# Second half of the output projection with tokens on the partitions, six raw weight buffers, and weight loads issued by ScalarE, in a fp32r decoder block

## The chip, the core and the metric

One Trainium2 chip, one core. The metric is the device time of one execution of the program, in microseconds (us). The kernel before takes 1840.0 us, the median of three runs (1839.93, 1840.0 and 1843.25). The engines are TensorE (PE, with PEld for its weight loads), VectorE (DVE), ScalarE (ACT), GpSimd (POOL) and SyncE (SP, which here only issues transfers).

## What is computed

One decoder block on 1024 tokens of width 2048, in float32. The input projection has 6528 columns; they feed an RWKV-7 group (16 heads, a recurrence over tokens) and a sliding-window attention group (16 heads). Their gated outputs are concatenated (2048 wide), go through the output projection, are added to x, and a final RMSNorm runs over the 2048 channels of each token. Cut to what matters here:

```
h = rmsnorm(x, norm_gain)
proj = h @ w_in                                   # 2048 x 6528
y_rwkv = rwkv7_group(proj[..., :4224], ...)
y_attn = swa_sink_alibi_group(proj[..., 4224:], sinks)
mix = concatenate([y_rwkv, y_attn])               # 1024 x 2048
x = x + mix @ w_out                               # 2048 x 2048
return rmsnorm(x, final_gain)
```

## The kernel before, in words

Tokens are worked on in two halves of 512. Everything is channel-major: channels lie on the 128 partitions, tokens on the free axis. A projection is cut into column tiles of 128 channels (51 for each half of the input projection, 16 for each half of the output projection, 134 in all), and each tile into four quarters of the contraction. One quarter is one weight piece of 128 x 512 (256 KB) and 12 matmuls of 512 columns: each fp32 product is made of three fp32r products (high x high, high x low, low x high), so both x and the weights are split into a rounded high part and the remainder. There are 536 quarters, numbered gq in the order in which PE takes them; 4 phases (input projection of half 0 and 1, output projection of half 0 and 1) begin at quarters 0, 204, 408 and 472. Constants: `START` is 12, `base(j)` the first quarter of interval j (24 quarters; 16 intervals, one per pair of heads and half), and `at` the quarter counted from there.

All engines run the same loop over gq, each through its own list of instructions, and are coupled by semaphores alone:

- SP (`load_w`, L365 to L370) issues the load of quarter gq+6 into one of three raw buffers. It waits until VectorE has made the low part of the piece that lay there (`w_ready`). SP also issues all other loads and stores, in program order with these.
- ScalarE (`high`, L581) makes the rounded part of quarter gq+4: it waits for the landed piece (`w_landed`) and for a free pair of split buffers, five of them, so it is at most four quarters ahead of PE (`w_used`).
- VectorE (`low`, L806) makes the remainder (`w_ready`), PE (`quarter`, L1230) waits for it.
- Between these stand the other parts of the block: `channels(j, at)`, `recurrence(j - 1, at)`, and `slices`, which split the x of a new phase (L587, L811) in groups of four chunks every second quarter. Around the state recurrence, `chain` (at 20 to 24) alternates between a small matmul on PE (L1511) and a copy on ScalarE (L729 to L733), eight times in an interval.

At the start, PE needs the mean square of the tokens of half 0: ScalarE squares x rows (L598), VectorE spreads the sums (L866), PE multiplies by a matrix of 1/2048 (L1523, at quarter 11), ScalarE takes the root (L610), VectorE the reciprocal (L872), and only then can tiles be read out of PSUM. At quarter 15 PE multiplies by the small LoRA matrices (L1263), which need the tanh of the first tile (L619); ScalarE's two sigmoids of these products (L632, L635) stand at quarter 14 of its list, and PE's transposes of the value tile (L1228, quarter 16) wait for the second.

At the end of each half of the output projection the 16 tiles (128 channels x 512 tokens) are read out and added to x (`add`, L1147), squared on ScalarE (L740), summed on GpSimd (L554 to L556) and over partitions on PE, and scaled (L1161) and stored. For half 1 this stands behind the last matmul: square, column sums by 8 matmuls (L1544), root (L747), reciprocal, a turn back to channel layout (L1228), 16 scalings and 16 stores.

## Time and profile before

| | |
|---|---|
| median of three runs | 1840.0 us (1839.93 to 1843.25) |
| the profiled execution | 1838.38 us, of which the span is 1836.5 us |
| PE busy | 1806.4 us (98%) |
| DVE busy | 1240.2 us (68%) |
| ACT busy | 814.6 us (44%) |
| POOL busy | 481.6 us (26%) |
| mean granted TensorE clock | 0.996 |
| DMA, mean | 115 GB/s |

The page's first part gives busy time and share per engine. The timeline lists instructions in order of time: start, duration, engine, line, operation, tiles, count; in brackets stands how long the engine had been idle before it and what released it. A large matmul stands with 0.39 us, but the next starts about 0.23 us later: matmuls overlap, so spacing is read from starts. A name with q (SPq, ACTq, DVEq) is an engine's instruction queue: there an issue of a transfer occupies the queue for the time given.

### The profile page before, as it was taken

The page shows a single profiled execution, that of the slowest core. Times are in us where ns is not written, and L with a number is a line of the kernel's source. Part 1 is how long each engine was busy: PE and PEld are TensorE (multiplying, and loading weights), DVE is VectorE, ACT ScalarE, POOL GpSimd, SP SyncE. Part 2 cuts the span into 40 slices and gives each one's busy share as a digit, 9 for nine tenths or more (in the row PEclk, how much of TensorE's full clock was granted, in tenths as well). Part 3 has the DMA queues.
Part 4 walks back from the last instruction along what each step waited for, and adds up shares of the span by engine and source line. Part 5 has one row for each costly group of instructions (what it writes and reads, how often), then busy time and mean ns, then how long its engine had stood idle before and what let it go on. Part 6 is the DMA issues. An engine that isn't in the chain of part 4 may idle for free.

```text
span 1836.5 us, 37316 instructions
## 1 busy us (share of the span) xinstructions
PE 1806.4 (98%) x14530; PEld 1482.5 (81%) x14530; DVE 1240.2 (68%) x2240; ACT 814.6 (44%) x1682; POOL 481.6 (26%) x1096
## 2 busy tenths in 40 slices
PE   8999999999999999999999999999999999999996
PEld 6878888888888887888888888888888888888885
DVE  5876777776767777567777767777778764356433
ACT  7544435353535355444453535353544543242221
POOL 0014233241505060232332515060605051111110
PEclk9999999999999999999999999999999999999998
DMA  8633333333333335332333333333334543465443
GB/s 299 196 97 90 89 93 91 94 95 94 91 90 92 92 93 171 114 95 86 95 88 95 97 90 92 89 97 89 106 90 116 167 113 114 124 210 179 154 120 126
DMA packets 197840, 211.84 MB, mean 115 GB/s; under 512 B 98592, under 2 KB 103840, under 8 KB 197152
## 3 DMA queue, kind: packets, MB, share of 16 engines
q1 hardware_dynamic: 196800, 208.73, 39.6%
q8 instruction: 115, 1.88, 0.4%
q10 hardware_dynamic: 864, 0.73, 0.1%
q14 instruction: 61, 0.50, 0.1%
HBM read 187.37 MB, written 22.02 MB: 114 GB/s over the span
## 4 chain that ended last, share of the span: by engine, by line
PE 90%; DVE 3%; DMA 2%; POOL 1%; ACT 1%; issue 1%; SPq 0%; DVEq 0%; ACTq 0%; POOLq 0%
PE psum L1243 75%; PE psum L1228 3%; PE psum L1361 2%; PE psum L1301 2%; PE psum L1329 1%; PE psum L1511 1%; PE psum L1394 1%; PE psum L1475 1%; DMA work<-in_x_t 1%; PE psum L1482 1%; PE psum L1263 1%; POOL sub_t L534 1%; POOL sub_io L536 1%; PE psum L1464 1%; DVE w_lo L808 1%
## 5 line engine op out<-in xcount | busy, mean ns | idle before, releaser
L1243 PE MATMUL psum<-x_hi,w_hi 128*128 128x512 f32 x2144 | 864.5, 403 | 10.5 <-DVE x_lo L817 6.2
L1243 PE MATMUL psum<-x_hi,w_lo 128*128 128x512 f32 x2144 | 838.7, 391 | 0.0
L1243 PE MATMUL psum<-x_lo,w_hi 128*128 128x512 f32 x2144 | 838.2, 391 | 0.0
L808 DVE TENSOR_TENSOR w_lo<-w_raw,w_hi 128x512 fp32r<-128x512 f32 x536 | 376.2, 703 | 477.3 <-ACT w_hi L579 449.3
L579 ACT ACTIVATE w_hi<-w_raw 128x512 fp32r<-128x512 f32 x536 | 335.5, 629 | 734.0 <-PE psum L1243 639.2
L1243 PEld LDWEIGHTS psum<-x_hi,w_hi 128*128 128x128 f32 x2144 | 403.4, 188 | 105.9 <-DVE w_lo L808 10.1
L1243 PEld LDWEIGHTS psum<-x_hi,w_lo 128*128 128x128 f32 x2144 | 402.8, 188 | 87.5
L1243 PEld LDWEIGHTS psum<-x_lo,w_hi 128*128 128x128 f32 x2144 | 403.8, 188 | 76.8 <-issue 0.7
L534 POOL TENSOR_TENSOR sub_t<-sub_l,sub_io 128x60 f32<-128x60 f32 (+24 forms) x496 | 192.1, 387 | 850.5 <-DMA sub_l<-scratch_L 812.9
L536 POOL TENSOR_TENSOR sub_io<-sub_io,sub_t 128x60 f32<-128x60 f32 (+24 forms) x496 | 209.7, 423 | 38.9
L556 POOL TENSOR_TENSOR v<-v,kb 128x512 f32<-128x512 f32 x29 | 38.1, 1314 | 267.1 <-ACT kb L740 266.7
L579 ACT ACTIVATE states<-psum,pc 128x64 f32<-128x64 f32 x112 | 35.0, 313 | 95.2 <-PE psum L1511 95.0
L579 ACT ACTIVATE late<-psum 64x256 f32<-64x256 f32 (+2 forms) x128 | 58.2, 482 | 1.1
L1511 PEld LDWEIGHTS psum<-states,score 128*128 128x128 f32 x256 | 47.9, 188 | 12.6 <-ACT states L579 1.9
L660 ACT ACTIVATE score<-score,top 128x192 f32<-128x192 f32 x128 | 56.5, 443 | 2.6 <-DVEq L1016 1.6
L933 DVE RECIPROCAL work<-work 128x512 f32<-128x512 f32 x16 | 53.6, 3353 | 2.2
L826 DVE TENSOR_TENSOR raw<-psum,rms 128x512 f32<-128x512 f32 x68 | 46.7, 686 | 3.4
L1511 PE MATMUL psum<-states,score 128*128 128x64 f32 x256 | 42.4, 247 | 0.7 <-ACT states L579 0.5
L984 DVE TENSOR_TENSOR late<-psum,cst 128x512 f32<-128x512 f32 x64 | 41.1, 684 | 2.4
L525 POOL COPY sub_io<-sub_ident 128x256 f32<-128x256 f32 x16 | 6.5, 406 | 125.3 <-PE psum L1403 107.0
L999 DVE SCALAR_TENSOR_TENSOR score<-cst,psum 128x192 f32<-128x192 f32 x128 | 36.6, 348 | 3.4 <-DVE ym L1138 3.4
L842 DVE SCALAR_TENSOR_TENSOR work<-work,par,raw 128x512 f32<-128x512 f32 x48 | 36.1, 752 | 1.7
(249 smaller groups left out, 1833.7 us busy)
## 6 DMA issues: line engine op xcount, KB each, us to landing
w_raw<-in_w_in SPq DMA_DIRECT2D x408, 256.0 KB, 2.7
w_raw<-in_w_out SPq DMA_DIRECT2D x128, 256.0 KB, 2.7
sub_l<-scratch_L SPq DMA_DIRECT2D x16, 384.0 KB, 4.1
stage<-in_x_t SPq DMA_DIRECT2D x20, 256.0 KB, 4.4
stage<-scratch_MIX SPq DMA_DIRECT2D x19, 256.0 KB, 4.0
late<-in_x_t SPq DMA_DIRECT2D x16, 256.0 KB, 3.7
scratch_MIX<-sa SPq DMA_DIRECT2D x16, 256.0 KB, 3.5
scratch_MIX<-ym SPq DMA_DIRECT2D x16, 256.0 KB, 3.2
```

The lines of the kernel that those rows point to most:

```text
L534: then(nc.gpsimd.tensor_tensor(t, left, right, ALU.mult))
L536: then(nc.gpsimd.tensor_tensor(rows, rows, t, ALU.subtract))
L556: then(nc.gpsimd.tensor_tensor(c_acc[:], c_acc[:], c_sq[u % 2], ALU.add))
L579: return nc.scalar.activation(dst, src, ACT.Copy, scale=scale)
L660: nc.scalar.activation(prob[:, x], prob[:, x], ACT.Exp, bias=top[:, 1, x:x + 1], accum_out=top[:, 2, x:x + 1])
L808: nc.vector.tensor_tensor(w_lo[gq % SPLIT][:], w_raw[gq % RAW][:], w_hi[gq % SPLIT][:].bitcast(F32), ALU.subtract).then_inc(w_ready, 1)
L826: then(nc.vector.tensor_tensor(dst, psum[:, bank_of(s)], rms[s // H1][:], ALU.mult))
L933: then(nc.vector.reciprocal(grow, grow))
L984: ins = nc.vector.tensor_tensor(am[:, 2 * half:2 * half + 2, hh].rearrange("p b c x t -> p b (c x t)"), psum[:, bank].rearrange("p (b t) - ...
L1228: return nc.tensor.transpose(dst, src, const("ident"))
L1243: mm = nc.tensor.matmul(psum[:, bank_of(s)], wt[gq % SPLIT][:, cols], xx[:, c], start=(c == 0 and wt is w_hi and xx is x_hi), stop=(c == K ...
L1511: nc.tensor.matmul(psum[:, 6, m * HD:(m + 1) * HD], mt[:, m], states[:, m], start=False, stop=True, skip_group_check=True).then_inc(state_ ...
```

## The change

Five edits come together.

1. Weight loads. From the fourth tile on (quarter 12 and later) ScalarE issues them, in its own list, ahead of `high(gq + 4)`. SP keeps the loads of the first three tiles. From quarter `WIDE` (492) on there are six raw buffers instead of three (the three staging buffers of x are then free), and loads are issued nine quarters ahead. What each load waits for is the low part of quarter gq+3 in either case.
2. The output projection of half 1 has tokens on the partitions: x is now the 128 x 128 stationary operand, and 512 columns of w_out move. Units are (column block of 512, chunk of the contraction): three passes of 16 units with four token blocks (12 matmuls each) and two passes of 16 units with two token blocks (6 matmuls each), so 80 units in place of 64 quarters, with 768 matmuls as before. A row's sum of squares comes from the accumulator of ScalarE's Square; root and reciprocal are on 128x1 columns; the gain row is multiplied on GpSimd for three column blocks.
3. x of phases 1 to 3 is split in pairs of chunks every quarter, in place of four chunks every second one.
4. The mean matmul of half 0 stands ahead of quarter 12 in place of quarter 11.
5. In the recurrence: the 32 matmuls of L1464 and L1467 are issued in two rounds of four, each in the order `TURNS`. And VectorE reads the R tile (`evicted`) ahead of the products that wait for `kkt_full`, not behind them.

The diff, cut to its core:

```diff
+ROWS = 4 * OUT1
+PASSES = [(cb, range(TBS)) for cb in range(CBS - 1)] + [(CBS - 1, (0, 1)), (CBS - 1, (2, 3))]
+LAST_UNITS = 4
+QUARTERS = ROWS + KC * len(PASSES)
+ADDED_AT = [ROWS + KC * (at + 1) + 1 + 2 * i for at, (_, tbs) in enumerate(PASSES[:-1]) for i in range(len(tbs))]
+FIRST_SCALED = ADDED_AT[-1] + 1
+WIDE, WIDE_RAW = 3 * ((ROWS + KC) // 3 + 1), 6
...
+        def loaded_by(gq):
+            return min(QUARTERS - 1, gq + 6 + (WIDE_RAW - RAW if gq + 6 >= WIDE + RAW - 1 else 0))
...
             @block.sync
                 for gq in range(QUARTERS):
-                    if START <= gq + 6 < QUARTERS:
-                        load_w(gq + 6)
...
             @block.scalar
+                def load_w(gq):
+                    slot = raw_of(gq)[0]
+                    if gq >= WIDE + WIDE_RAW:
+                        act.wait_ge(w_ready, gq - WIDE_RAW + 1)
+                    elif slot >= RAW:
+                        act.wait_ge(x_ready, 4 * KC)
+                    else:
+                        act.wait_ge(w_ready, gq - RAW + 1)
...
+                    nc.scalar.dma_start(w_raw[slot][:], src).then_inc(w_landed[slot], 16)
...
+                    for ahead in range(loaded_by(gq - 1) + 1, loaded_by(gq) + 1):
+                        if ahead >= START:
+                            load_w(ahead)
                     if START <= gq + 4 < QUARTERS:
                         high(gq + 4)
...
+                    if gq in ADDED_AT:
+                        square_rows(ADDED_AT.index(gq))
+                    if gq == FIRST_SCALED:
+                        root_rows(0)
+                        root_rows(1)
+                    if gq - FIRST_SCALED in (1, 2):
+                        scale_rows(gq - FIRST_SCALED - 1)
+                for tb in (2, 3):
+                    square_rows(PIECES.index((CBS - 1, tb)))
+                    root_rows(tb)
+                    scale_rows(tb)
...
             @block.vector
+                def add_rows(n):
+                    cb, tb = PIECES[n]
...
+                    nc.vector.tensor_tensor(row_piece[tb][cb], psum[:, row_bank(cb, tb)], x_in[n % 2], ALU.add
+                                            ).then_inc(row_read, 1)
...
             @block.tensor
-                    if gq == START - 1:
+                    if gq == START:
...
+                def row_products(gq, tb, c, cb):
...
+                    nc.tensor.matmul(psum[:, bank], x_hi[:, c, tokens], hi[:], start=(c == 0), stop=False)
+                    nc.tensor.matmul(psum[:, bank], x_hi[:, c, tokens], lo[:], start=False, stop=False)
+                    return nc.tensor.matmul(psum[:, bank], x_lo[:, c, tokens], hi[:], start=False, stop=(c == KC - 1))
```

How instructions stand on the engines, in three places. First ScalarE's list near the start, from the last two squares of x rows to the root of the first mean (`rms0`); w_raw and w_hi with their numbers are the raw and the rounded weight buffers, `late` the squared x rows. Before:

```order
L598 ACTIVATE work,stat<-work 128x2048
L598 ACTIVATE late,stat<-late 128x2048
L579 ACTIVATE w_hi2<-w_raw0 128x512
L579 ACTIVATE w_hi3<-w_raw1 128x512
L610 ACT_TABLE_LOAD
L610 ACTIVATE rms0<-psum,eps 128x512
L579 ACTIVATE w_hi4<-w_raw2 128x512
```

and in the changed kernel, whose line numbers differ:

```order
L682 ACTIVATE late,stat<-late 128x2048
L662 DMA w_raw0<-in_w_in 128x512
L662 DMA w_raw1<-in_w_in 128x512
L662 DMA w_raw2<-in_w_in 128x512
L646 ACTIVATE w_hi2<-w_raw0 128x512
L662 DMA w_raw0<-in_w_in 128x512
L646 ACTIVATE w_hi3<-w_raw1 128x512
L694 ACT_TABLE_LOAD
L694 ACTIVATE rms0<-psum,eps 128x512
L662 DMA w_raw1<-in_w_in 128x512
L646 ACTIVATE w_hi4<-w_raw2 128x512
L662 DMA w_raw2<-in_w_in 128x512
```

The loads of quarters 12 to 14 stand behind the last square of x rows, and from quarter 15 on one load stands ahead of each rounding.

Second, ScalarE's list in the last pass of the output projection, where the sums of squares (`row_sums`), their roots (`stat`) and the first scalings come between the roundings of the weights. Before, the last tiles of half 1:

```order
L579 ACTIVATE w_hi0<-w_raw2 128x512
L579 ACTIVATE w_hi1<-w_raw0 128x512
L579 ACTIVATE w_hi2<-w_raw1 128x512
L579 ACTIVATE w_hi3<-w_raw2 128x512
L740 ACTIVATE kb<-score 128x512
L579 ACTIVATE w_hi4<-w_raw0 128x512
```

and in the changed kernel:

```order
L836 ACTIVATE kb,row_sums<-wr 128x512
L662 DMA stage1<-in_w_rows 128x512
L646 ACTIVATE w_hi2<-stage2 128x512
L662 DMA stage2<-in_w_rows 128x512
L646 ACTIVATE w_hi3<-w_raw0 128x512
L836 ACTIVATE kb,row_sums<-sub_io 128x512
L662 DMA w_raw0<-in_w_rows 128x512
L646 ACTIVATE w_hi4<-w_raw1 128x512
L841 ACTIVATE stat<-stat,eps 128x1 x2
L662 DMA w_raw1<-in_w_rows 128x512
L646 ACTIVATE w_hi0<-w_raw2 128x512
L646 ACTIVATE xt<-xt,stat 128x512
```

A load stands between each two roundings, and it waits for VectorE's remainder of the piece that was rounded just before it.

Third, VectorE's list at quarter 196 and 197 (the last interval of half 0), where `raw` is the buffer into which the R tile is read. Before:

```order
L808 TENSOR_TENSOR w_lo0<-w_raw2,w_hi0 128x512
L936 SCALAR_TENSOR_TENSOR work<-work,par 128x512
L938 TENSOR_TENSOR qr<-work,decay 128x4x64 x2
L826 TENSOR_TENSOR raw<-psum,rms0 128x512
L838 COPY carry<-raw 128x1
L808 TENSOR_TENSOR w_lo1<-w_raw0,w_hi1 128x512
```

and in the changed kernel:

```order
L921 TENSOR_TENSOR w_lo0<-w_raw2,w_hi0 128x512
L939 TENSOR_TENSOR raw<-psum,rms0 128x512
L951 COPY carry<-raw 128x1
L1051 SCALAR_TENSOR_TENSOR work<-work,par 128x512
L1053 TENSOR_TENSOR qr<-work,decay 128x4x64 x2
L921 TENSOR_TENSOR w_lo1<-w_raw0,w_hi1 128x512
```

The read of the tile has moved ahead of three instructions.

## Rows read from the trace of the kernel before

**Rows 1.** The page's first part: busy us, share, instructions.

```profile
PE 1806.4 (98%) x14530; PEld 1482.5 (81%) x14530; DVE 1240.2 (68%) x2240; ACT 814.6 (44%) x1682; POOL 481.6 (26%) x1096
```

**Rows 2.** Timeline of PE, where it waits: start, us, line, operation [idle before].

```profile
39.82 0.67 PE L1523 MATMUL psum<-v,cst 128*128 128x512 f32 x1 [1.80 <-DVE v L866]
...
693.73 0.50 PE L1243 MATMUL psum<-x_hi,w_hi 128*128 128x512 f32 x1 [2.81 <-DVEq L830]
...
712.11 0.44 PE L1511 MATMUL psum<-states,score 128*128 128x64 f32 x2 [0.51 <-ACT states L579]
...
1419.65 0.50 PE L1243 MATMUL psum<-x_hi,w_hi 128*128 128x512 f32 x1 [0.55 <-DVEq L830]
...
1642.97 0.50 PE L1243 MATMUL psum<-x_hi,w_hi 128*128 128x512 f32 x1 [0.92 <-DVE late L1147]
```

**Rows 3.** Timeline behind the last large matmul, PE, DVE, ACT and SP.

```profile
1817.90 0.39 PE L1243 MATMUL psum<-x_hi,w_lo 128*128 128x512 f32 x1
...
1818.33 0.69 DVE L1147 TENSOR_TENSOR pt<-psum,decay 128x512 f32<-128x512 f32 x1 [10.19 <-PE psum L1243]
1819.05 0.63 ACT L740 ACTIVATE kb<-pt 128x512 f32<-128x512 f32 x1 [10.25 <-DVE pt L1147]
...
1820.83 0.26 ACT L747 ACTIVATE part<-psum,eps 128x4 f32<-128x4 f32 x1 [1.14 <-PE psum L1544]
1821.12 0.18 DVE L1155 RECIPROCAL part<-part 128x4 f32<-128x4 f32 x1 [2.10 <-ACT part L747]
...
1823.02 0.75 DVE L1161 SCALAR_TENSOR_TENSOR xt<-xt,fgain,psum 128x512 f32<-128x512 f32 x1 [1.26 <-PE psum L1228]
...
1832.24 1.40 DVE L1161 SCALAR_TENSOR_TENSOR pt<-pt,fgain,psum 128x512 f32<-128x512 f32 x2
1833.01 0.99 SPq L473 DMA_DIRECT2D out<-pt  x2
```

**Rows 4.** Timeline of PE in the recurrence of interval 15.

```profile
1422.61 0.69 PE L1394 MATMUL psum<-zs,xt 64*64 64x64 f32 x32
1423.12 0.39 PE L1394 MATMUL psum<-kkt,xt 64*64 64x64 f32 x13
...
1426.65 0.36 PE L1464 MATMUL psum<-late,wr 64*64 64x64 f32 x8
...
1427.88 0.34 PE L1475 MATMUL psum<-late 128*64 128x64 f32 x4
```

**Rows 5.** Timeline near the start: one piece rounded, its remainder, the next load.

```profile
3.69 0.63 ACT L579 ACTIVATE w_hi<-w_raw 128x512 fp32r<-128x512 f32 x1 [1.01 <-DMA w_raw<-in_w_in]
...
4.36 0.69 DVE L808 TENSOR_TENSOR w_lo<-w_raw,w_hi 128x512 fp32r<-128x512 f32 x1 [2.68 <-ACT w_hi L579]
...
5.08 0.33 SPq L370 DMA_DIRECT2D w_raw<-in_w_in  x1
```

**Rows 6.** Timeline of ACT, DVE and PE, 37 to 56 us.

```profile
37.66 1.13 ACT L579 ACTIVATE w_hi<-w_raw 128x512 fp32r<-128x512 f32 x2
...
41.67 3.35 DVE L872 RECIPROCAL rms<-rms 128x512 f32<-128x512 f32 x1 [1.40 <-ACT rms L610]
...
51.16 1.28 ACT L632 ACT_TABLE_LOAD   x1
...
52.39 0.69 DVE L808 TENSOR_TENSOR w_lo<-w_raw,w_hi 128x512 fp32r<-128x512 f32 x1
...
53.49 0.68 ACT L635 ACTIVATE work<-psum,par 128x512 f32<-128x512 f32 x1
...
55.68 0.60 PE L1228 MATMUL psum<-cst,raw 128*128 128x128 f32 x4
```

**Rows 7.** The page's DMA issues: KB of one, median us from issue to landing.

```profile
w_raw<-in_w_in SPq DMA_DIRECT2D x408, 256.0 KB, 2.7
```

**Rows 8.** Waits of ACT and of SP's queue: us in total, times, longest.

```profile
ACT states L579 <- PE psum L1511: 95.0, 101, 1.3
...
SPq L370 <- DVE w_lo L808: 1216.2, 468, 7.3
```

More of the change, by code:

```diff
@@ L159, in slices_before, with row_bank @@
     return 1 + (i >= values_before(1)) + (i >= values_before(2))
+def row_bank(cb, tb):
+    return (0 if cb % 2 else 4) + tb
 def us_rows(c):
@@ L285, in program @@
                       pt[:, 0], pt[:, 1]]]
+        row_piece = [[xn[1][CBS * tb + cb] for cb in range(CBS)] for tb in range(TBS)]
+        row_inv = stat[:, 0, 0:TBS]
         psum = ctx.enter_context(nc.psum_tensor("psum", [P, 8, HALF], F32))
@@ L291, in program @@
         ident_landed = sem("ident_landed")
-        w_landed = [sem(f"w_landed{i}") for i in range(RAW)]
+        w_landed = [sem(f"w_landed{i}") for i in range(WIDE_RAW)]
         x_landed = [sem(f"x_landed{i}") for i in range(STAGE)]
@@ L352, in current, with chunk_pair @@
             return [(j, gq - base(j)) for j in range(INTERVALS + 1) if 0 <= gq - base(j) < TAIL]
-        def chunk_group(gq):
+        def chunk_pair(gq):
             for ph in range(1, 4):
-                group, odd = divmod(gq - (4 * FIRST[ph] - 6), 2)
-                if 0 <= group < 4 and not odd:
-                    return ph, group
+                pair = gq - (4 * FIRST[ph] - 6)
+                if 0 <= pair < KC // 2:
+                    return ph, 2 * pair, 2
             return None
@@ L557, in accumulate, with gain_rows @@
                     pool.sem_inc(c_summed, 1)
+                def gain_rows(cb):
+                    pool.wait_ge(row_gain_landed, 16)
+                    for tb in range(TBS):
+                        pool.wait_ge(row_squared, TBS * cb + tb + 1)
+                        piece = row_piece[tb][cb]
+                        nc.gpsimd.tensor_tensor(piece, piece, gain_row[:, cb * HALF:(cb + 1) * HALF], ALU.mult
+                                                ).then_inc(row_gained, 1)
                 nc.gpsimd.memset(xt[:], 0.0)
@@ L571, in _ @@
                                 clear(j - 1)
-                    for u in range(2 * KC - 1):
+                    for u in range(KC):
                         if gq == done(OUT0 + u) + 1:
                             accumulate(u)
+                    for at in range(CBS - 1):
+                        if gq == ROWS + KC * (at + 1):
+                            gain_rows(at)
             @block.scalar
@@ L788, in _ @@
                             channels(j, at)
-                    for u in range(2 * KC - 1):
+                    for u in range(KC):
                         if gq == done(OUT0 + u) + 1:
                             square(u)
-                    if gq == 4 * OUT1 + 5:
-                        root(0)
-                square(2 * KC - 1)
-                root(1)
+                    if gq == ROWS + 5:
+                        root()
+                    if gq in ADDED_AT:
[9 more added lines that the diff above has]
+                    scale_rows(tb)
             @block.vector
@@ L1536, in between @@
                                 chain(j - 1, 2 * (at - 20))
-                    quarter(gq, between)
-                pe.wait_ge(c_summed, 2 * KC - 1)
-                for last, squared in enumerate((c_acc[:], c_sq[(2 * KC - 1) % 2])):
-                    if last:
-                        pe.wait_ge(c_squared, 2 * KC)
-                    for b in range(NB):
-                        mm = nc.tensor.matmul(psum[:, 2, b:b + 1], squared[:, b * P:(b + 1) * P], const("mean")[:, 0:1],
-                                              start=(not last and b == 0), stop=bool(last), skip_group_check=True)
-                mm.then_inc(mean_done, 1)
-                pe.wait_ge(c_spread, 1)
-                for b in range(NB):
-                    mm = turn(psum[:, 3, b * P:(b + 1) * P], rms[0][:, b * P:(b + 1) * P])
-                mm.then_inc(c_turned, 1)
+                    if gq < ROWS:
+                        quarter(gq, between)
+                    else:
+                        rows(gq)
+                last_rows()
 SCRATCH = {
```

303 lines of the change are left out of this document (209 added, 94 removed).

## The prediction, made before the changed kernel was run

> **What bounds the kernel now.** I read the engines' shares first, then the places where PE waits, then the chain behind the last matmul, and last the rows of ScalarE and VectorE around the weight pieces. PE is busy for 1806.4 of 1836.5 us [rows 1], and large matmuls of the last phase start 0.228 us apart: (1817.90 - 1642.97) / 767 for its 768 [rows 2, 3]. So nothing that VectorE, ScalarE or a transfer does faster counts, unless PE waits for it. PE waits in few places: behind the start 1.80 us for the first mean, 2.81 and 0.55 us for a tile to be read at the end of each half's last interval, 0.51 us for a state copy, 0.92 us at the start of the last phase [rows 2]. The other idle time is at the end: the last matmul ends at 1818.3, the span at 1836.5, so 18.2 us hold one tile's way through add, square, sum, root and reciprocal, and then 16 scalings and stores [rows 3]. The question is thus which PE waits go, which ones come, and how long the end becomes. I work from the profiled execution, 1838.38 us, 1.6 us below the median of 1840.0, and add the 1.6 us at the end.
>
> **The end.** With tokens on the partitions the last unit leaves only four 128x512 pieces to finish, two of them already summed. Behind the last matmul: add 0.7 (L1147's 0.69), square with its accumulator 0.75 (L740's 0.63 and an estimated 0.1 for reading the sum), sum, root 0.26, reciprocal 0.18 and the hops between, 0.8 together, then two scalings on ScalarE, 1.2, beside two on VectorE: 3.5 us. SP issues each store in 0.33 (0.99 for the overlapping pair and wait at 1833.01), so the last of four issues starts at about 4.0; before, the last one started near 1833.67 and the span ended 2.8 later [rows 3]. That makes 6.8 us in place of 18.2: **-11.4**, with 5.8 to 8.5 as its bounds (landings side by side, or one issue behind another).
>
> **PE waits that go.** VectorE now reads the R tile straight behind the remainder of quarter 200, ahead of three instructions, and the load of that quarter is not stuck in SP's list, so I take both waits of 2.81 and 0.55 as gone; behind them PE next needs quarter 197's piece, long ready. The first pass of the last phase writes four fresh banks and doesn't wait for a tile to be added: 0.92 goes. Pairs of chunks halve the block of splits that held up the state copy: 0.51 goes. Together **-4.8** (bounds -3.4 to -4.8).
>
> **The recurrence.** The 32 matmuls of L1464 and L1467 take 1427.88 - 1426.65 = 1.23 us in each interval. They alternate pairs on the same 64x64 corner of the array. The 16 matmuls of L1394, issued in the order TURNS, take 0.51 [rows 4], so 32 would take 1.02. The difference of 0.21 times 16 intervals is **-3.4** (bounds 0 and -3.4).
>
> **Loads on ScalarE, in the middle.** An issue occupies a queue for 0.33 us [rows 5]: some 540 of them are 178 us more on an engine busy for 814.6 [rows 1], so there is room on average. What hurts is order. SP's queue waits 1216.2 us, in 468 waits, for remainders that VectorE has not yet made [rows 8]; this wait now stands in ScalarE's list, ahead of the rounding of quarter gq+4 and whatever follows. Laid side by side, the 536 roundings and remainders of before show that the remainder of quarter gq+3 is mostly done when ScalarE gets there; it is late by more than the issue at the fifth quarter of each interval (about 1.2 us, with over 2 us of ScalarE idling behind it) and at the 22nd of every fourth (1.2 to 1.6 us). In the state chain ScalarE waits for PE 0.94 us per copy (95.0 / 101) [rows 8], which covers the 0.33; and PE, once a copy is made, needs it only about 0.9 later. I take **0**, with 0 to +10 as bounds.
>
> The Trainium skill, page DMA: Bandwidth & Descriptors, section Issuing engines are not separate DMA queues, says that transfers issued by different engines run on the same 16 DMA engines and interleave; by that rule only issue time can be saved, which here is SP's, on which nothing waits, and the edit would be worth nothing. The row of 1216.2 us says more than the rule does: the wait moves as well.
>
> **The start.** Here the order costs. Before, SP issued the load of quarter 12 long before ScalarE needed it, and ScalarE rounded it at 37.66 right behind the last square [rows 6]. Now the load is issued behind that square, at about 36.9 (I assume that the queue is some 0.8 ahead of the engine), and lands 2.7 later [rows 7], at 39.7. Rounding and remainder (1.4) and the spreading of the sums (0.7) put the mean matmul at 41.9 in place of 39.82 [rows 2]. PE has quarter 11 to do meanwhile, so its wait is only about 1.1. The table load ahead of the root is no longer hidden: the reciprocal starts at 44.2, not 41.67, and ends 2.5 late. Behind it stand in VectorE's list the remainders of 14 and 15, the first tile, remainder 16, the keys, remainder 17. Before, remainder 17 ended at 53.08 [rows 6]; now it is 2.5 later, and 0.9 more, since the rounding of 15 stands behind a load that waits for remainder 14: 56.5. ScalarE's two sigmoids stand behind the load that waits for this one: issue 0.35, rounding 0.63, a square 0.6, table load 1.28, sigmoids 1.35: 60.7. PE's transposes of the value tile need the second sigmoid, and started at 55.68 [rows 6]; now 60.8: **+5.1**. The bounds are +1.4 (only the tanh ahead of quarter 15 late) and +8.
>
> **The last two passes.** A unit has six matmuls, 1.37 us. Its piece must be rounded, its remainder made, and now a load issued, before the next piece can be rounded, since the load waits for that remainder: from 3.69 to 5.41 us these three take 1.72 [rows 5], 1.75 with the hop back. So rounding, remainder and issue run one behind the other, slower than PE. Where VectorE adds a finished piece and ScalarE squares it, the step is 1.38 to the remainder, 0.6 for the add, 0.75 for the square: 2.7. Count from the start of unit 520, PE's first short one, when the piece of 524 is rounded: up to 544 there are 14 steps of 1.75 and 6 of 2.7 (four adds in the fourth pass, two in the fifth), 40.7 us. Roots and reciprocals make the next step 2.25, two scalings the next 1.8; the remainder of 547 stands behind VectorE's scalings and ends at 48.0, and the last four follow 0.6 apart: 50.4. PE would be at its last four units after 28 x 1.365 = 38.2 us. So it waits **+12.2** in small pieces from about the tenth short unit on. Bounds: 0, if ScalarE's issue and wait overlap with its work, and +16, if an issue takes 0.45 and a square 0.8. The lead of four pieces is in the count already. The three passes before have units of 2.74 us, above the mean of 1.75 and 2.7 to 3.6, and cost nothing.
>
> **Sum.** -11.4 - 4.8 - 3.4 + 5.1 + 12.2 = -2.3: 1836.1 by the profiled execution, 1837.7 as a median. Two large terms of either sign nearly cancel, which is why the range is wide.
>
> **Rivals.**
> 1. *The last passes don't run in step.* For it: no row of before shows ScalarE waiting at an issue in mid-stream, and VectorE is 68% busy only [rows 1]. Against it: the load stands ahead of the next rounding in the list, and waits for a remainder made only after the last one. It would give 1837.7 - 12.2 = 1825.5.
> 2. *The start stays covered.* If ScalarE's queue gets its loads out earlier, during the squares, the term of 5.1 shrinks to about 1: 1833.5. Against it: the three loads stand behind the last square, which starts only when its rows have landed.
> 3. *The state chain falls behind (slower).* Each interval has eight copies in a row on ScalarE, with a load and a rounding between them. If VectorE's remainders come so much later than now that a load holds ScalarE for more than the 0.94 us of slack in a copy [rows 8], PE waits in each interval; it decides from about 1 us of delay at one copy. Half a microsecond to one in 15 intervals is 7 to 15 us: 1845 to 1853, say 1848. For it: delays of 1.2 to 1.6 in three intervals already. Against it: there the copy would come some 0.8 late, still inside the slack.
>
> **Chances.** The forecast 0.52 (own range 1833.5 to 1842.5), rival 1 0.18, rival 2 0.12, rival 3 0.18. About 0.2%, 3.7 us, is what a measurement can tell from no change. Faster, below 1836.3: both first rivals mostly (0.27), and a fifth of the forecast: 0.38. Slower, above 1843.7: rival 3, and a twentieth of the forecast: 0.21. Same: 0.41. The range of 1826 to 1846 leaves out most of rival 3's upper part and half of rival 1.
>
> **What the new profile would show.** The end: 6 to 8 us between the last large matmul and the span's end. The start: the mean matmul near 42, the transposes of the value tile near 61 with 3 to 5 us of PE idle before them. The middle: no wait of more than 0.6 us for a tile read at the ends of the halves, 1.0 us for the 32 matmuls. The last two passes: a sum of PE waits for remainders of 10 to 15 us, roundings 1.75 us apart, each behind a load issue. I am wrong if PE has no gaps there (rival 1), or if PE waits for state copies in every interval (rival 3).

## The result, and the profile after

The changed kernel takes 1846.05 us, the median of nine runs (1845.61 to 1848.12), beside 1840.0 us before, the median of nine runs as well (1836.39 to 1843.25). The ratio is 1.0035, with 95% interval 1.0025 to 1.0045: 0.35% slower, where 1837.7 us had been forecast. The profiled execution took 1847.35 us; its span is 1845.2 us, 8.7 us longer than the 1836.5 before. The mean granted TensorE clock is 0.997, as before 0.996, so the difference is not one of the clock as a whole. The two profiled executions lie on opposite sides of their medians (1.3 us above it after, 1.6 us below it before), so what is read from the traces below adds up to 8.7 us where the medians are 6.1 us apart.

The busy times of the engines answer to [rows 1]:

```profile
PE 1811.9 (98%) x14510; PEld 1477.4 (80%) x14510; DVE 1252.5 (68%) x2254; ACT 840.0 (46%) x1725; POOL 479.2 (26%) x1093
```

PE's share is the same and says nothing. The places where it waits do. These are the waits of PE after (line and tile, what was waited for: us in total, times, longest):

```profile
PE psum L1668 <- DVE w_lo L921: 9.2, 20, 1.6
...
PE psum L1378 <- ACT work L719: 3.8, 1, 3.8
PE psum L1413 <- issue: 1.9, 1, 1.9
PE psum L1378 <- DVEq L1101: 1.3, 1, 1.3
PE psum L1434 <- DVEq L1070: 1.2, 1, 1.2
```

L1668 is the first of the three matmuls of a token block in the last phase (`row_products`), L1378 the transposes, L1413 the LoRA matmuls of quarter 15. The waits of [rows 2] (1.80, 2.81, 0.51, 0.55, 0.92 us) are not there any more. In their place stand 20 small waits for remainders in the last two passes, two at the start, of 1.9 us at L1413 (PE is done with quarter 14 at 51.4, and the tanh that it needs then ends at 53.1) and of 3.8 us for the second sigmoid, and two of just over 1 us later on, of which the one at L1434 had been 0.65 before.

To see what each is worth, I took the start of the same work on PE in both traces and subtracted: after minus before, in us.

| PE starts | shift |
|---|---|
| quarter 16 | +5.88 |
| quarter 17 | +8.08 |
| last phase (quarter 472) | +3.51 |
| last two passes (unit 520; before, the matmul 576 of the phase) | +3.34 |
| last large matmul | +18.87 |
| end of the span | +8.7 |

So the start costs 8.1, the whole middle gives back 4.6, the last two passes cost 15.5, and the end gives back 10.2.

**The start.** Timeline of all engines after, 36 to 61 us (start, duration, engine, line, tiles; in brackets the idle time before and what ended it); it answers to [rows 6]:

```profile
36.77 1.30 ACTq L662 DMA_DIRECT2D w_raw<-in_w_in  x3
...
39.64 0.63 ACT L646 ACTIVATE w_hi<-w_raw 128x512 fp32r<-128x512 f32 x1 [0.93 <-DMA w_raw<-in_w_in]
...
41.81 1.10 PE L1711 MATMUL psum<-v,cst 128*128 128x512 f32 x2
...
44.20 3.35 DVE L985 RECIPROCAL rms<-rms 128x512 f32<-128x512 f32 x1 [1.31 <-ACT rms L694]
```

```profile
56.86 0.34 ACTq L662 DMA_DIRECT2D w_raw<-in_w_in  x1
57.30 0.63 ACT L646 ACTIVATE w_hi<-w_raw 128x512 fp32r<-128x512 f32 x1 [2.98 <-DVE w_lo L921]
...
58.47 1.28 ACT L716 ACT_TABLE_LOAD   x1
...
60.35 0.68 ACT L719 ACTIVATE work<-psum,par 128x512 f32<-128x512 f32 x1
```

The load at 56.86 stands behind a remainder, and ScalarE has been idle 2.98 us in front of it. Then follow the rounding, a square, the table load and the sigmoids, as forecast. PE's side of it:

```profile
61.17 1.09 PE L1378 MATMUL psum<-cst,raw 128*128 128x128 f32 x4 [3.81 <-ACT work L719]
61.91 0.78 PE L1393 MATMUL psum<-x_hi,w_hi 128*128 128x512 f32 x1
...
62.91 0.63 PE L1393 MATMUL psum<-x_hi,w_lo 128*128 128x512 f32 x1
63.34 0.63 PE L1393 MATMUL psum<-x_hi,w_hi 128*128 128x512 f32 x1
```

Behind the idle time the matmuls start 0.43 us apart, not 0.23, and eleven of them do so, so quarter 16 takes 5.03 us in place of 2.83. The columns of the next view are stretch, length, busy time and instructions of PE, PEld, DVE, ACT and POOL, granted clock, DMA share and GB/s:

```profile
61.50:66.50 5.00, 5.00 (x15) 4.03 (x14) 3.81 (x5) 4.04 (x7) 0.00 (x0) 0.50 0.44 129
66.50:71.50 5.00, 5.00 (x24) 4.11 (x23) 4.00 (x7) 4.02 (x7) 0.00 (x0) 0.99 0.60 188
```

PE is "busy" for all 5.00 us in both, but with 15 matmuls in one and 24 in the other: the granted clock is 0.50, the 1.2 GHz level, behind the 3.81 us of idling, and 0.99, the 2.4 GHz level, later. The wait costs more than its own length. How much more varies: in the runs below that leave this part of the lists as it is, quarter 16 took 4.41, 4.42, 4.43 and 5.22 us behind the same wait of 3.8 us, that is 1.6 to 2.4 us too much, and quarter 17 started 6.3 to 7.3 us later than before. So of the +8.08 of this execution 1 to 2 us are its own: its first matmuls, too, ran slowly for longer than those of before, which makes quarter 4 1.2 us late.

**The last two passes.** Timeline after, in unit 520's pass and behind:

```profile
1797.99 0.61 ACT L646 ACTIVATE w_hi<-w_raw 128x512 fp32r<-128x512 f32 x1
...
1798.16 1.26 POOL L620 TENSOR_TENSOR pt<-pt,kw 128x512 f32<-128x512 f32 x1 [3.81 <-ACT kb L836]
1798.63 1.33 DVE L921 TENSOR_TENSOR w_lo<-w_raw,w_hi 128x512 fp32r<-128x512 f32 x1 [1.31 <-ACT w_hi L646]
1800.00 0.33 ACTq L662 DMA_DIRECT2D w_raw<-in_w_rows  x1
...
1800.02 0.50 PE L1668 MATMUL psum<-w_hi,x_hi 128*128 128x512 f32 x1 [1.59 <-DVE w_lo L921]
...
1800.44 0.63 ACT L646 ACTIVATE w_hi<-w_raw 128x512 fp32r<-128x512 f32 x1 [1.83 <-DVE w_lo L921]
...
1801.10 0.69 DVE L921 TENSOR_TENSOR w_lo<-w_raw,w_hi 128x512 fp32r<-128x512 f32 x1 [1.13 <-ACT w_hi L646]
...
1801.83 0.33 ACTq L662 DMA_DIRECT2D w_raw<-in_w_rows  x1
...
1801.85 0.50 PE L1668 MATMUL psum<-w_hi,x_hi 128*128 128x512 f32 x1 [0.17 <-DVE w_lo L921]
...
1802.26 0.63 ACT L646 ACTIVATE w_hi<-stage 128x512 fp32r<-128x512 f32 x1 [1.19 <-DVE w_lo L921]
```

Rounding 1800.44, remainder 1801.10, issue 1801.83, next rounding 1802.26: the step is 1.82 us, and neither ScalarE nor VectorE is busy for it (they idle 1.19 and 1.13 us of each). PE starts a unit when the remainder is there, 1.82 to 1.83 apart, though its six matmuls need 1.37. The view puts only 0.17 us of these 0.45 down as idle time, since a matmul stands with 0.39 us; the 9.2 us of waits are thus less than what the passes lose. And one remainder takes 1.33 us instead of 0.69, beside the multiply by the gain row on GpSimd (L620).

**The end.** Timeline behind the last large matmul, answering to [rows 3]:

```profile
1836.77 0.39 PE L1670 MATMUL psum<-w_hi,x_lo 128*128 128x512 f32 x1
...
1837.19 0.69 DVE L1273 TENSOR_TENSOR pt<-psum,decay 128x512 f32<-128x512 f32 x1
...
1839.48 1.34 ACT L646 ACTIVATE score<-score,stat 128x512 f32<-128x512 f32 x2 [0.29 <-DVEq L1283]
...
1841.11 0.45 SPq L522 DMA_DIRECT2D out_rows<-score  x1
1841.60 0.45 SPq L522 DMA_DIRECT2D out_rows<-pt  x1
```

From 1837.16 to 1845.2 are 8.0 us in place of 18.2.

### The profile page after: what moved, and what is told of

Same layout as the page of the kernel before. It is cut to its first block, busy times and chain, and to the rows that moved or that the text cites. A ratio compares the mean times of both kernels' runs of the same rounds, so it can differ in the third digit from the quotient of the medians.

```text
span 1845.2 us, 37370 instructions
## 1 busy us (share of the span) xinstructions
PE 1811.9 (98%) x14510; PEld 1477.4 (80%) x14510; DVE 1252.5 (68%) x2254; ACT 840.0 (46%) x1725; POOL 479.2 (26%) x1093
## 4 chain that ended last, share of the span: by engine, by line
PE 91%; DVE 4%; ACT 2%; DMA 2%; issue 1%; ACTq 0%; DVEq 0%; SPq 0%
PE psum L1393 67%; PE psum L1378 3%; PE psum L1668 3%; PE psum L1670 3%; PE psum L1669 3%; PE psum L1511 2%; PE psum L1451 2%; DVE w_lo L921 1%; PE psum L1479 1%; PE psum L1660 1%; PE psum L1544 1%; ACT w_hi L646 1%; PE psum L1624 1%; DMA work<-in_x_t 1%; PE psum L1631 1%
## 5 line engine op out<-in xcount | busy, mean ns | idle before, releaser
L1393 PE MATMUL psum<-x_hi,w_hi 128*128 128x512 f32 x1888 | 765.2, 405 | 6.6 <-DVE x_lo L930 6.3
L1393 PE MATMUL psum<-x_hi,w_lo 128*128 128x512 f32 x1888 | 739.6, 392 | 0.0
L1393 PE MATMUL psum<-x_lo,w_hi 128*128 128x512 f32 x1888 | 737.6, 391 | 0.0
L1393 PEld LDWEIGHTS psum<-x_hi,w_hi 128*128 128x128 f32 x1888 | 356.0, 189 | 91.6 <-issue 18.9
L1668 PE MATMUL psum<-w_hi,x_hi 128*128 128x512 f32 x256 | 102.4, 400 | 9.3 <-DVE w_lo L921 9.2
L1669 PE MATMUL psum<-w_lo,x_hi 128*128 128x512 f32 x256 | 99.8, 390 | 0.0
L1670 PE MATMUL psum<-w_hi,x_lo 128*128 128x512 f32 x256 | 99.8, 390 | 0.0
L1668 PEld LDWEIGHTS psum<-w_hi,x_hi 128*128 128x128 f32 x256 | 48.0, 188 | 27.9 <-DVE w_lo L921 18.4
L1670 PEld LDWEIGHTS psum<-w_hi,x_lo 128*128 128x128 f32 x256 | 48.1, 188 | 10.1
L1669 PEld LDWEIGHTS psum<-w_lo,x_hi 128*128 128x128 f32 x256 | 48.1, 188 | 9.5 <-issue 0.2
```

The lines of the kernel that those rows point to most:

```text
L1393: mm = nc.tensor.matmul(psum[:, bank_of(s)], wt[gq % SPLIT][:, cols], xx[:, c], start=(c == 0 and wt is w_hi and xx is x_hi), stop=(c == K ...
L1668: nc.tensor.matmul(psum[:, bank], x_hi[:, c, tokens], hi[:], start=(c == 0), stop=False)
L1669: nc.tensor.matmul(psum[:, bank], x_hi[:, c, tokens], lo[:], start=False, stop=False)
L1670: return nc.tensor.matmul(psum[:, bank], x_lo[:, c, tokens], hi[:], start=False, stop=(c == KC - 1))
```

## The experiments

Two theories stood against each other. *Wait*: what costs is that the load's wait for a remainder stands ahead of the next rounding in ScalarE's list. *Issue*: what costs is the time of some 540 issues on an engine that is needed elsewhere. The runs were made on several chips, each beside runs of the kernel before, whose medians there were 1839.4 to 1842.1 us; two runs are therefore compared by their ratios where a few microseconds matter. In what follows, "short units" is the time that PE takes for the 32 units of six matmuls of the last two passes; before, the same 192 matmuls took 43.3 us, after 58.8.

**All weight loads on SP.** The rest of the change alone. SP has after's `load_w` in its loop, ScalarE none:

```diff
-                        if ahead >= START:
+                        if ahead >= START and False:   # the same loop on SP, with "not"
```

> All weight loads are issued by SP again, everything else as in the changed kernel. Theory A (the place of the loads in ScalarE's list costs, at the start and in the two passes of short units): the 8.1 us lost by quarter 17 and most of the 15.5 us lost in the last two passes come back, 1846 - 8 - 14 = 1824 us. Rival B (units of six matmuls are too short for rounding, remainder, add and square in themselves, whoever issues the loads): only the start comes back, 1838 us, and PE still waits for remainders from unit 530 on.

Measured: 1825.69 us (1824.57 to 1829.26), ratio to before 0.9915 (0.99 to 0.9931). The short units take 45.6 us, quarter 17 starts at 59.57, 7.4 earlier than after. PE's and ScalarE's waits:

```profile
PE psum L1563 <- DVEq L1191: 3.0, 4, 1.2
PE psum L1687 <- DVE w_lo L940: 1.4, 3, 0.8
```

```profile
ACT w_hi L665 <- DMA w_raw<-in_w_in: 101.1, 37, 6.7
```

So the rest of the change makes the kernel 0.85% faster, and issuing the loads from ScalarE takes 20 us away again (1.2%, or 22 us, by the ratios). The second fence shows the cost of SP's list: 37 times ScalarE waits for a piece that has not landed, up to 6.7 us, since the load stood behind other transfers (the load behind the longest wait was issued at 339.95, right behind the transfers of `scratch_X` and `scratch_XT`, and landed at 342.93); PE feels only the 3.0 us at L1563 and a few more.

**SP for the last phase only.** ScalarE keeps the loads up to there:

```diff
-                        if ahead >= START:
+                        if ahead >= START and ahead < ROWS:   # SP: the others
```

> ScalarE issues the loads of quarters 12 to 471, SP those of the output projection of half 1. Theory A: the last two passes lose at most 1 to 2 us, the start keeps its 8 us: 1846 - 14 = 1832 us. Rival B: no change, 1846 us.

Measured: 1833.52 us (1832.83 to 1837.3), ratio 0.9959 (0.9943 to 0.9975). Short units 45.6 us; the wait at the start is still 3.85. The last phase by itself is worth 13.2 us of the 20.

**SP for the start only.** Loads up to quarter 47 on SP:

```diff
-                        if ahead >= START:
+                        if ahead >= START and ahead >= 48:   # SP: the others
```

> SP issues the loads up to quarter 47, ScalarE all later ones. Theory A: the transposes of the value tile start near 56 us instead of 61.2 and without a 3.8 us wait, no stretch at 1.2 GHz behind them; the last passes stay as they are: 1846 - 8 = 1838 us. Rival C (the start is late by the later mean matmul, not by the loads): still above 1844 us.

Measured: 1838.52 us (1837.44 to 1843.15), ratio 0.9985 (0.9975 to 0.9994). PE in this kernel waits only 0.48 us ahead of the transposes, and its matmuls behind them are 0.23 us apart; quarter 17 starts at 58.20, 0.66 earlier than before. The short units stay at 58.8. The two places are independent: what the two runs gain by their medians, 12.5 and 7.5 us, adds up to the 20.4 of all loads on SP. With the end's 10 they account for the sign.

**The same number of issues, the wait moved by one place.** All loads stay on ScalarE; the load stands behind the rounding of gq+4, not ahead of it:

```diff
-                    for ahead in range(loaded_by(gq - 1) + 1, loaded_by(gq) + 1):
-                        if ahead >= START:
-                            load_w(ahead)
                     if START <= gq + 4 < QUARTERS:
                         high(gq + 4)
+                    for ahead in range(loaded_by(gq - 1) + 1, loaded_by(gq) + 1):
+                        if ahead >= START:
+                            load_w(ahead)
```

> ScalarE still issues the loads, but each stands behind the rounding of quarter gq+4 instead of ahead of it; it waits for the same remainder. Theory A (what costs is a wait for the last remainder ahead of the next rounding, not the issuing engine): the last two passes take about 46 us in place of 58.8, at the start the rounding of 15 no longer waits for remainder 14 (1 us earlier): 1846 - 13 - 1 = 1832 us. Rival D (the 0.33 us issues on ScalarE themselves are too much beside 1.37 us units): the last two passes stay above 54 us and the time above 1841 us.

Measured: 1827.84 us (1826.78 to 1833.82), ratio 0.994 (0.9921 to 0.996). Short units 45.6 us. The time is 4 us better than expected. The wait at the start is 3.3 instead of 3.8, that of 1.9 at L1413 shrinks to 0.3, and quarter 17 is 3.6 late instead of 8.1; and between quarter 17 and the last phase PE needs 2.8 us less than after (1576.8 against 1579.5). Of these 2.8, 0.57 are the wait at L1434, which is back to 0.66. Of the rest, 2.0 come in pieces of 0.17 us, one in each of 12 intervals: with the load ahead of the rounding ScalarE's second sigmoid starts 0.24 us later there, and PE's transposes of the keys behind it 0.14 us later. Waits of PE, and ScalarE and VectorE in the last passes:

```profile
PE psum L1668 <- DVE w_lo L921: 1.2, 2, 0.8
```

```profile
1798.53 0.61 ACT L646 ACTIVATE w_hi<-stage 128x512 fp32r<-128x512 f32 x1
...
1799.05 0.62 ACT L646 ACTIVATE w_hi<-w_raw 128x512 fp32r<-128x512 f32 x1
...
1799.17 0.69 DVE L921 TENSOR_TENSOR w_lo<-stage,w_hi 128x512 fp32r<-128x512 f32 x1 [1.31 <-ACT w_hi L646]
...
1799.78 0.68 DVE L921 TENSOR_TENSOR w_lo<-w_raw,w_hi 128x512 fp32r<-128x512 f32 x1
1799.90 0.33 ACTq L662 DMA_DIRECT2D stage<-in_w_rows  x1
```

Two roundings run back to back, and so do two remainders: the lead is made up after each hold-up. Since ScalarE still issues as many loads, each in 0.33 us, *Issue* falls, and *Wait* stands: 13.3 us in the last passes, 4.5 at the start and 2.8 between, which is the whole difference of the two spans (1845.2 against 1824.6).

**One load less ahead.** The same test by one number: in the wide phase loads are issued eight quarters ahead instead of nine, so each waits for the remainder of gq+2, which is older:

```diff
-            return min(QUARTERS - 1, gq + 6 + (WIDE_RAW - RAW if gq + 6 >= WIDE + RAW - 1 else 0))
+            return min(QUARTERS - 1, gq + 6 + (WIDE_RAW - RAW - 1 if gq + 6 >= WIDE + RAW - 1 else 0))
```

> The changed kernel with one number changed: with six buffers, ScalarE's loads run eight quarters ahead, not nine, and still stand ahead of the rounding of quarter gq+4. So each waits for the remainder of gq+2, not of gq+3. Theory A (the step in the last passes is rounding, remainder and issue one behind the other because of this wait): the last two passes take about 46 us, not 58.8: 1846 - 13 = 1833 us. Rival H (the place of the issue ahead of the rounding is what costs, 0.33 us a unit and more): 54 us or more, 1841 us.

Measured: 1833.63 us (1831.96 to 1834.69), ratio 0.9965 (0.9952 to 0.9978), short units 45.7 us. PE's wait at the start is unchanged (3.8), and the last passes are free:

```profile
PE psum L1668 <- DVE w_lo L921: 1.4, 3, 0.9
```

A *later* load makes the kernel 13 us faster. Six buffers with loads nine ahead were tight by exactly the one piece whose remainder was still being made.

**Before, with its loads issued by ScalarE.** The move alone: `load_w(gq + 6)` goes from SP's loop to ScalarE's, ahead of `high(gq + 4)`.

```diff
 (SP)                if START <= gq + 6 < QUARTERS:
-                        load_w(gq + 6)
 (ScalarE)
+                    if START <= gq + 6 < QUARTERS:
+                        load_w(gq + 6)
                     if START <= gq + 4 < QUARTERS:
                         high(gq + 4)
```

> The kernel before with one edit: its loads from quarter 12 on are issued by ScalarE, ahead of the rounding. Theory A: the start loses about 8 us (wait for the second sigmoid and a stretch at half clock), the last phase with its long quarters nothing, and one wait of 2.8 us at the end of half 0 shrinks or stays: 1846 to 1848 us. Rival B: 1840 us, as before.

Measured: 1843.94 us (1842.52 to 1847.97), ratio 1.0013 (1.0003 to 1.0022), so the move alone costs 2.4 us beside the kernel before in the same series (1842.05), and the expected 1846 to 1848 was too much. Quarter 17 is 6.14 late (a wait of 3.3 us and slow matmuls behind it), and the wait of 2.81 us at the end of the first half shrinks to 0.50, since that load is no longer held up in SP's list. With no short units there is no loss at the end. The traces of the two kernels differ by 4.8 us in their spans; why the medians differ by less stays open.

**PE kept busy in the wait at the start.** 14 matmuls more, into a bank that is not in use, ahead of the transposes that wait:

```diff
+                        if j == 0:
+                            for _ in range(14):
+                                nc.tensor.matmul(psum[:, 5], x_hi[:, 0, 0:P], x_hi[:, 0], start=True, stop=True)
                         pe.wait_ge(va_raw, h + 1)
                         pe.wait_ge(sigma_a, j + 1)
```

> The changed kernel, with 14 further matmuls of 512 columns into an unused bank before PE waits for the second sigmoid of the first interval, some 3.2 of the 3.8 us. Theory A (the slow matmuls behind that wait are the clock, which fell while PE was idle): the 11 matmuls 0.43 us apart behind the wait become 0.23 us apart, quarter 17 starts 2.2 us earlier: 1844 us. Rival E (they are slow for another reason, operands or banks): quarter 17 starts when it did, 1846 us.

Measured: 1845.4 us (1844.76 to 1846.49), ratio 1.0022 (1.0011 to 1.0032). PE at the start:

```profile
56.08 3.33 PE L1419 MATMUL psum<-x_hi 128*128 128x512 f32 x14
60.09 0.63 PE L1378 MATMUL psum<-cst,raw 128*128 128x128 f32 x4 [0.67 <-ACT work L719]
...
60.78 0.40 PE L1393 MATMUL psum<-x_lo,w_hi 128*128 128x512 f32 x1
61.02 0.40 PE L1393 MATMUL psum<-x_hi,w_lo 128*128 128x512 f32 x1
```

Quarter 16 to 17 takes 2.85 us in place of 5.03, and the granted clock of 60.4 to 63.4 is 1.00. So 2.2 us of the start are the clock, brought on by the idle time (1.6 to 2.4 in the other executions with that wait). In the profiled execution a wait of 1.8 us for a transfer in the middle took most of it back; 1844 had been expected, and the two intervals of the ratio overlap (1.0025 to 1.0045 after); the effect is shown in the trace, not in the time.

**GpSimd's multiply cut to one column.** The multiply by the gain row covers 1 column of 512 here; the gain of the other columns is left out.

```diff
-                        piece = row_piece[tb][cb]
-                        nc.gpsimd.tensor_tensor(piece, piece, gain_row[:, cb * HALF:(cb + 1) * HALF], ALU.mult
+                        piece = row_piece[tb][cb][:, 0:1]
+                        nc.gpsimd.tensor_tensor(piece, piece, gain_row[:, cb * HALF:cb * HALF + 1], ALU.mult
```

> The changed kernel with the gain multiplication of three column blocks on GpSimd cut to one column of 512 (the rest of that gain is left out), all waits kept. Theory F (VectorE's remainder takes 1.35 to 1.43 us instead of 0.69 while GpSimd multiplies, four times in the last passes): each of the four becomes 0.69, and the last two passes take 58.8 - 2.8 = 56 us: 1843 us. Rival: the long remainders come from something else and stay: 1846 us.

Measured: 1843.43 us (1842.19 to 1845.28), ratio 1.0014 (1.0004 to 1.0023). The short units take 56.2 us, 2.6 less, and the remainder just behind the start of the multiply, which now takes 0.19 us, is back to its own time:

```profile
1785.57 0.19 POOL L620 TENSOR_TENSOR sub_l<-sub_l,kw 128x1 f32<-128x1 f32 x1 [4.18 <-ACT kb L836]
...
1786.05 0.69 DVE L921 TENSOR_TENSOR w_lo<-stage,w_hi 128x512 fp32r<-128x512 f32 x1 [1.31 <-ACT w_hi L646]
```

It happens four times in the short units, 0.64 to 0.74 each: 2.6 us, and it counts in full only because rounding, remainder and issue run in one chain. The Trainium skill, SBUF — State Buffer, section Who interferes with whom, says that a VectorE instruction with two inputs in SBUF contends with a GpSimd instruction that reads SBUF; this trace agrees (0.69 against 1.33 us), and in the order of the load behind the rounding (short units of 45.6 with the multiply in full) the same contention costs nearly nothing.

**The old order of the recurrence's matmuls.** The loops of L1464 and L1467 as before, without `TURNS`:

```diff
-                            for c, hh in TURNS:
+                            for hh in range(2):
+                                for c in range(2):
```

> The changed kernel with the 32 recurrence matmuls in their old order. They took 1.23 us before and 1.09 now: by that alone 16 x 0.14 = 2.2 us more, 1848 us. My forecast had 3.4 us for this edit, 1849.5 us. If the order only shifts a wait, no change.

Measured: 1848.12 us (1847.68 to 1851.93), ratio 1.0049 (1.0029 to 1.0068), beside 1.0035 after: 2 us or so slower, and the intervals overlap, so by the times alone neither 0 nor 3.4 is excluded. The traces decide it. After, the sequence runs from 1430.65 to 1431.74:

```profile
1430.65 0.34 PE L1612 MATMUL psum<-late,wr 64*64 64x64 f32 x8
...
1431.74 1.15 PE L1624 MATMUL psum<-late 128*64 128x64 f32 x32
```

In the old order it takes 1.24 us again (1430.85 to 1432.09). From quarter 17 to the last phase PE then needs 1581.7 us beside 1579.5 after, 2.2 more, 0.14 in each of the 16 quarters in which these matmuls stand. The profiled spans (1845.6 beside 1845.2) hide it, since that execution reached quarter 17 1.7 us earlier. So the order is worth 2.2 us.

**ScalarE in the middle only.** SP up to quarter 47 and for the last phase, ScalarE for 48 to 471, ahead of the rounding as in the change:

```diff
-                        if ahead >= START:
+                        if ahead >= START and 48 <= ahead < ROWS:   # SP: the others
```

> SP issues the loads up to quarter 47 and those of the output projection of half 1, ScalarE the ones between (48 to 471). Theory A: no loss at the start, 46 us in the last two passes, and in the middle the waits of PE that the kernel with all loads on SP has (late transfers behind other work in SP's list, 1 us each at 346, 351, 693 and 697 us) are gone: 1825.7 - 4.7 = 1821 us. Rival G (with the loads on SP the middle was no slower): 1825 us.

Measured: 1825.51 us (1824.64 to 1827.3), ratio 0.9918 (0.9903 to 0.9933); 1821 had been expected, so this is a miss. The 4.7 us had been read from the profiled execution of all loads on SP, which was the slowest of its four (1829.26, the others 1824.57 to 1826.26). ScalarE's wait for landed pieces falls from 101.1 us to 7.5, and one for remainders stands in its place:

```profile
ACT w_hi L665 <- DVE w_lo L940: 58.8, 44, 3.4
```

With 424 loads on either engine the ratio is 0.9918 or 0.9915: in the middle it does not matter for the time who issues. (Where the load stands does: behind the rounding the middle took 2.8 us less.) The Trainium skill, DMA: Bandwidth & Descriptors, section Issuing engines are not separate DMA queues, says that only issue time can be saved so; in the middle the two runs agree. Over the whole kernel they don't: by that rule all on SP and all on ScalarE would be alike, and they are 20 us apart, because the waits ahead of the issues move too.

**The best of these together.** SP up to quarter 47, then ScalarE with the load behind the rounding, and ScalarE storing the last two pieces that it has scaled itself:

```diff
+                    if START <= gq + 4 < QUARTERS:
+                        high(gq + 4)
                     for ahead in range(loaded_by(gq - 1) + 1, loaded_by(gq) + 1):
-                        if ahead >= START:
+                        if ahead >= START and ahead >= 48:   # SP: the others
                             load_w(ahead)
-                    if START <= gq + 4 < QUARTERS:
-                        high(gq + 4)
...
+                for cb in range(2):
+                    act.wait_ge(scaled_by_act, 2 * 3 + cb + 1)
+                    nc.scalar.dma_start(io["out_rows"][3 * P:4 * P, cb * HALF:(cb + 1) * HALF], row_piece[3][cb]
+                                        ).then_inc(out_stored, 16)
```

> SP issues the loads up to quarter 47, ScalarE the later ones, each behind the rounding of quarter gq+4; and ScalarE issues the stores of its own last two pieces. From the kernel with the loads behind the rounding (1827.8): the start gives back 3.6 us less a slower or faster first ramp, the end 0.5 to 0.9 us since four issues in a row on SP become two and two: 1823.5 us.

Measured: 1823.74 us (1822.26 to 1825.58), ratio 0.9911 (0.9896 to 0.9926), the lowest of all kernels here, though its interval and that of all loads on SP overlap. It beats both kernels. The two queues at the end:

```profile
1813.16 0.39 PE L1693 MATMUL psum<-w_hi,x_lo 128*128 128x512 f32 x1
...
1816.45 0.99 SPq L538 DMA_DIRECT2D out_rows<-pt  x2
1816.63 0.96 ACTq L930 DMA_DIRECT2D out_rows<-score  x2
```

The last issues end 4.0 us behind the last matmul (1817.59 against 1813.55) instead of 4.9, yet the span still ends 8.3 us behind it, against 8.0 after: the gain of 0.5 to 0.9 us did not come. The issues of these four stores with their size and the time from issue to landing:

```profile
out_rows<-pt SPq DMA_DIRECT2D x2, 256.0 KB, 3.4
out_rows<-score ACTq DMA_DIRECT2D x2, 256.0 KB, 3.8
```

After, the same two views had 3.0 and 2.7 us. One by one the four land at 1819.44, 1820.11, 1820.82 and 1821.42, 3.0, 3.5, 3.7 and 4.2 us behind their issues: the issues moved together, the landings still come 0.6 to 0.7 us apart, as they did after (1842.69, 1843.39, 1844.11, 1844.78). So what ends the kernel here is one piece landing behind another, and earlier issues on a second queue did not help.

## Why the prediction was wrong

The mechanism of the two large costs was the one forecast; the sizes were not. The steps that failed are the price of PE's wait at the start (+5.1, measured +8.1), that of a unit in the last two passes (+12.2, measured +15.5), and the loads in the middle, put at 0 and measured at +2.8. The forecast sum was -2.3, the sum from the two traces 8.7 (6.1 by the medians).

| term | predicted | measured |
|---|---|---|
| the end | -11.4 | -10.2 |
| PE waits that go | -4.8 | -5.9 |
| the recurrence | -3.4 | -2.2 |
| loads in the middle | 0 | +2.8 |
| the rest of the middle: a new wait of 1.2, less small pieces | 0 | +0.8 |
| the start | +5.1 | +8.1 |
| the passes of 12 matmuls | 0 | -0.2 |
| the last two passes | +12.2 | +15.5 |

- **The last two passes: right in kind, mis-sized by 3.3.** The roundings are in step with the issues, as forecast, and PE waits for remainders, 9.2 us in 20 waits by the view (10 to 15 forecast). The steps that failed: 1.75 per unit, which is 1.82 (about 1.0 us over the 14 steps counted), since there is also a hop of 0.1 from the issue to the next rounding; and the remainder at 0.69, which is 1.33 beside GpSimd's multiply. The second is 2.6 us of the 3.3; the two together are 0.3 more than that. I had counted that multiply as free, because it stands on an engine with time to spare. Rival 1's price of 12.2 was good: it is what the load behind the rounding gives back (13.3).
- **The start: every time up to the wait was right, the consequence was missing.** Mean matmul 41.81 (41.9 forecast), reciprocal 44.20 (44.2), transposes 61.17 (60.8). The forecast priced PE's wait at its length. The 2.2 us at half clock behind it were missing, and so was a slower first run-up: 13 slow matmuls instead of 7 at the very start, 1.2 us at quarter 4. That second part varies between kernels with the same start and has no cause that I can name, and the first varies too, so part of the 3.0 is this execution's: in the four others with these lists the start cost 6.3 to 7.3. The forecast also left the late tanh out of what it expected to see; it is the wait of 1.9 us at L1413, inside the time up to the transposes.
- **The recurrence: mis-sized.** The 32 matmuls take 1.09 us in place of 1.23 [rows 4] (1430.65 to 1431.74), 0.14 per interval and not 0.21, 2.2 us in all, as the run with the old order shows. The pace was taken from the 16 matmuls of L1394; why the 32 don't reach it was not tested.
- **The middle: 0 was too low, and rival 3 did not come.** PE waits for the state copies no more than before. What failed is the step that looked at the state copies alone: a load ahead of the rounding also holds up ScalarE's sigmoids, and PE's transposes behind the second one cost 0.17 us more in 12 intervals, 2.0 us. They do so in every kernel whose loads stand ahead of the rounding there, and in none with the loads behind it or on SP. The wait at L1434 grew from 0.65 to 1.22 us, and only where ScalarE issues the loads of the start, ahead of the rounding. With this and some smaller pieces the middle takes 2.8 us more than with the loads behind the rounding. Besides, there is a wait of 1.3 us for a tile that VectorE reads. It (L1378 behind L1101) is in every version with the rest of the change, wherever its loads are issued, and not in before with loads on ScalarE, so it belongs to another of the edits. Which one was not tried.
- **The waits that go: right.** All four are gone; the gain is 1.1 larger.
- **The end: right within its bounds (5.8 to 8.5, measured 8.0).** The last issue starts 4.4 us behind the matmul, not 4.0, since issues in a row take 0.45 and not 0.33, and 3.6 us follow it, not 2.8.

**The range.** Its upper end rested on rival 3 alone, although the start's bound was +8 and that of the last passes +16; with both at their bounds and nothing else changed the sum is 4.4, or 1844.4, and the recurrence at its bound of 0 gives 1847.8. Both large costs came to about their bounds (8.1 and 15.5). The forecast's own range, 1833.5 to 1842.5, was narrower than its terms allowed.

## What to carry to other kernels

Before a transfer is moved to a busy engine's list, look at what the transfer waits for, not at what its issue costs: a wait that is harmless in a list that does nothing else becomes a link between two producers that had overlapped. Put such an issue behind the work that can go on without it, or issue it one buffer later; either gave 13 us in the last passes here, and the first another 7 elsewhere, for no more than an exchange of lines or a number. And price an idle time of PE like those of 3.3 to 3.9 us here with the slow stretch behind it (1.1 to 2.4 us), and an operation on GpSimd with what it does to VectorE where VectorE is in a chain.

## What was not expected of the hardware

- PE idle for 3.81 us came back at the 1.2 GHz level for eleven matmuls of 512 columns (0.43 us apart, granted clock 0.50), 2.2 us; in three other kernels the transposes behind the same wait still ran at full pace (0.63 us for the four, not 1.09), and seven or eight matmuls then were slow, 1.6 us. With the idle time cut to 0.67 us the granted clock stayed at 1.00. Idle times of 1.80 and 2.81 us had left it up before [rows 2].
- A 128x512 subtraction on VectorE with both inputs in SBUF took 0.69 us alone and 1.33 to 1.43 beside a 128x512 multiply of 1.28 us on GpSimd.
- An issue of a transfer occupies a queue for 0.33 us alone and 0.43 to 0.5 in a row, on SP as on ScalarE.
- The last four stores of 256 KB landed 0.6 to 0.7 us apart whether one queue issued them or two, and the last one landed 3.2 us behind its issue with one queue and 4.2 with two.
